# Compressed branch of the attention heads: its bias added by VectorE from the selected branch's table, and each tile of queries takes only the blocks that end within it

## The reference, cut to what matters

```python
end = arange(n_cmp) * CMP_STRIDE + CMP_LEN - 1          # 31 blocks: 31, 47, ..., 511
dist = qpos[:, None] - end[None, :]
vis = dist >= 0
bias = rel_bias[rel_bucket(dist)]
s = einsum('bqgrd,bngd->bgrqn', qg, kc) * SCALE + bias
p = softmax(where(vis, s, NEG_INF)); p = where(any(vis), p, 0)
o = einsum('bgrqn,bngd->bqgrd', p, vc)
```

## Time and profile before

| | us |
|---|---|
| median of three executions | 2705.33 (2705.25 to 2711.46) |
| the profiled execution, whole | 2703.42 |
| its span | 2701.6 |
| PE busy | 2542.1 (94%) |
| DVE busy | 896.3 (33%) |
| ACT busy | 750.1 (28%) |
| POOL busy | 422.2 (16%) |
| stretch of the 8 turns of `heads`, about | 1316 to 2325 |

### The profile page before, as it was taken

How to read it: one execution, slowest core, us unless ns; L and a number is a source line. 1 busy time by engine, 2 the same in 40 slices (tenths; PEclk the granted TensorE clock), 3 DMA queues, 4 the chain that set the end, 5 groups by cost and what they waited for, 6 DMA issues and landing times.

```text
span 2701.6 us, 49851 instructions
## 1 busy us (share of the span) xinstructions
PE 2542.1 (94%) x20936; PEld 2349.6 (87%) x20936; DVE 896.3 (33%) x1560; ACT 750.1 (28%) x1266; POOL 422.2 (16%) x577
## 2 busy tenths in 40 slices
PE   7998999999999999968899999999999999876996
PEld 6987888988999999968899898989899999655996
DVE  1235112221633533322433324242433333332334
ACT  1124111112422411111432324333333333221223
POOL 1002000950000000332311112020202011111000
PEclk9998999999999999989899999999999999987998
DMA  9986776766454365699523232323222232466221
GB/s 322 330 280 220 234 228 197 227 215 216 157 154 140 126 218 180 166 79 113 119 63 89 63 89 66 90 61 92 80 76 82 71 88 64 157 210 247 94 93 64
DMA packets 321990, 395.72 MB, mean 146 GB/s; under 512 B 24846, under 2 KB 283166, under 8 KB 319906
## 3 DMA queue, kind: packets, MB, share of 16 engines
q1 hardware_dynamic: 301650, 327.66, 40.8%
q0 software_dynamic: 20144, 65.12, 8.6%
HBM read 372.03 MB, written 43.72 MB: 154 GB/s over the span
## 4 chain that ended last, share of the span: by engine, by line
PE 85%; DMA 6%; DVE 4%; issue 2%; ACT 2%; SPq 1%; POOL 0%; DVEq 0%; ACTq 0%; POOLq 0%
PE acc L1898 64%; PE work L1819 4%; DMA raw<-in_w_kv 3%; PE out_acc L2073 3%; PE work L1766 2%; PE work L2042 2%; PE work L1807 2%; PE work L2059 1%; PE acc L1766 1%; PE work L2036 1%; PE work L2035 1%; SPq L565 1%; PE out_acc L2070 1%; DMA ada<-in_w_ada 1%; DVE normed L1386 1%
## 5 line engine op out<-in xcount | busy, mean ns | idle before, releaser
L1898 PE MATMUL acc<-h_hi,w_hi 128*128 128x260 f32 x4896 | 1017.1, 289 | 53.8 <-DVE w_lo L1259 42.4
L1898 PE MATMUL acc<-h_hi,w_lo 128*128 128x260 f32 x4896 | 995.5, 285 | 0.0
L1898 PE MATMUL acc<-h_lo,w_hi 128*128 128x260 f32 x4896 | 994.3, 285 | 0.0
L1898 PEld LDWEIGHTS acc<-h_hi,w_hi 128*128 128x128 f32 x4896 | 764.1, 191 | 95.1 <-issue 57.8
L1259 DVE TENSOR_TENSOR w_lo<-raw,w_hi 128x1024 fp32r<-128x1024 f32 (+1 forms) x316 | 403.6, 1278 | 1134.4 <-ACT w_hi L921 1129.6
L1898 PEld LDWEIGHTS acc<-h_hi,w_lo 128*128 128x128 f32 x4896 | 764.8, 191 | 0.0
L1898 PEld LDWEIGHTS acc<-h_lo,w_hi 128*128 128x128 f32 x4896 | 763.7, 191 | 0.0
L921 ACT ACTIVATE w_hi<-raw 128x1024 fp32r<-128x1024 f32 (+1 forms) x316 | 332.5, 1053 | 1209.3 <-PE acc L1898 1147.2
L861 POOL TENSOR_TENSOR probs<-probs,row_stats 128x128 f32<-128x128 f32 (+3 forms) x128 | 111.0, 898 | 475.5 <-DVE row_stats L1612 475.5
L1819 PE MATMUL work<-rows_T_early,w_c_early 128*128 128x124 f32 x960 | 111.9, 275 | 0.7 <-ACT rows_T_early L965 0.7
L1819 PEld LDWEIGHTS work<-rows_T_early,w_c_early 128*128 128x128 f32 x960 | 109.5, 192 | 1.1 <-DVE rows_T_early L1332 1.1
(11 more groups left out here) (319 smaller groups left out, 2010.3 us busy)
## 6 DMA issues: line engine op xcount, KB each, us to landing
ada<-in_w_ada SPq DMA_DIRECT2D x192, 512.0 KB, 4.8
raw<-in_w_in_b SPq DMA_DIRECT2D x128, 512.0 KB, 3.9
raw<-in_w_in_a SPq DMA_DIRECT2D x64, 512.0 KB, 5.0
raw<-in_w_kv SPq DMA_DIRECT2D x48, 512.0 KB, 5.0
raw<-in_w_out_a SPq DMA_DIRECT2D x32, 512.0 KB, 3.6
raw<-in_w_out_b SPq DMA_DIRECT2D x32, 512.0 KB, 3.3
x_scr<-x POOLq DMA_DIRECT2D x2, 4160.0 KB, 14.4
pages_early<-in_cache_k_cmp SPq DMA_DIRECT2D x32, 256.0 KB, 4.1
```

Of the source, the lines that this page charges most:

```text
L1898: last = mm_(out[half][0:n, 0:HT], part[slot][:, kk, cols_], src[:, k, half * HT:(half + 1) * HT], start=(first and part is HI and src is ...
```

## The change

The bias tables of the compressed branch go: the buffer `BC`, its DRAM table `c_scr`, the DMA that writes it and the DMA that loads it in each turn. The loads that a turn waits for are four instead of five. PE's compressed scores are four matmuls a head instead of eight, without the bias, with 7, 15, 23 and 31 columns. DVE fills the probabilities with -1e30, adds the bias to each tile's columns out of `BH` at every 16th column, and takes maximum and difference from SBUF instead of PSUM.

```diff
-        BC = place("bias_cmp", [NCMP, 2, TP])
...
-            pool.dma_start(c_scr, bass.AP(tensor=g_scr.tensor, offset=GLEN + 481, ap=[[2 * GLEN, NH], [-16, NCMP], [1, TP]])).then_inc(s_bscr, 16)
...
-            pool.wait_ge(s_bscr, 16 * (1 + NH // 4))
+            pool.wait_ge(s_bscr, 16 * (NH // 4))
...
-                pool.dma_start(BC[:, :, :], h2(c_scr)).then_inc(hd_in, 16)
...
-                    dve.wait_ge(hd_in, 80 * (i + 1))
+                    dve.wait_ge(hd_in, 64 * (i + 1))
...
                 if u < 2:
-                    sc = S[0][:, 0:NT * NCMP].rearrange("p (t n) -> p t n", n=NCMP)
                     pr = PR[:, 0:NT * NCMP].rearrange("p (t n) -> p t n", n=NCMP)
-                    o(V.tensor_reduce(STAT[:, 0:4], sc, AX.X, ALU.max))
-                    V.tensor_tensor(pr, sc, STAT[:, 0:4].unsqueeze(2).broadcast_to([P, NT, NCMP]), ALU.subtract).then_inc(negm, 1)
+                    o(V.memset(PR[:, 0:NT * NCMP], NEG))
+                    for t in range(NT):
+                        w, at = 8 * t + 7, (3 - t) * P + CL - 1
+                        last = V.tensor_tensor(pr[:, t, 0:w], S[0][:, NCMP * t:NCMP * t + w], BH[:, hh, at:at + CS_ * (w - 1) + 1:CS_], ALU.add)
+                    o(last)
+                    o(V.tensor_reduce(STAT[:, 0:4], pr, AX.X, ALU.max))
+                    V.tensor_tensor(pr, pr, STAT[:, 0:4].unsqueeze(2).broadcast_to([P, NT, NCMP]), ALU.subtract).then_inc(negm, 1)
...
-                    pe.wait_ge(hd_in, 80 * (i + 1))
+                    pe.wait_ge(hd_in, 64 * (i + 1))
...
                     for t in range(NT):
-                        out = S[0][:, NCMP * t:NCMP * t + NCMP]
-                        mm_(out, BC[:, hh, P * t:P * t + P], ident[0:NCMP, 0:NCMP], start=True, stop=False)
-                        last = mm_(out, qs(t), kc, start=False, stop=True)
+                        w = 8 * t + 7
+                        last = mm_(S[0][:, NCMP * t:NCMP * t + w], qs(t), kc[:, 0:w], start=True, stop=True)
```

More of the change, by code:

```diff
@@ L391, in build @@
         b_scr = dram("b_scr", (NH, P, 512))
-        c_scr = dram("c_scr", (NH, NCMP, TP))
         x_scr = dram("x_scr", (P, KT * T))
```

## The result

The changed kernel took 2658.9 us (median of four, 2656.65 to 2664.92) against 2705.29 of the kernel before on the same chip: a ratio of 0.9827, 95% interval 0.9806 to 0.9849, 46.4 us less. The forecast was 2667, range 2661 to 2682. Two later comparisons gave 39.8 us (0.9854, 0.9832 to 0.9877) and 44.9 us (0.983, 0.9813 to 0.9848).

A forecast was written before the change was run, and what follows sets the result against it. PE, with 85% of the chain of waits, was taken as the bound. Scores 28.8 plus clock 9.2 gave 38.0 us off, other terms 0: 2665.4 for the profiled execution, 2667 for the median, range 2661 to 2682.

The forecast's parts named there:

- The scores: PE's compressed scores in `heads`: stretch falls from 2.69 to 0.89 us a head as row alternation goes, saving 28.8 us.
- the bound I gave for the columns: PE's scores: if fewer moving columns pay, 48 columns a head save 0.08 us, 1.3 us in all.
- The clock: PE behind the score stretches: all six falls to half clock go, 6 x 1.53 = 9.2 us; bounds 0 and 9.2.
- DVE: Added fill and adds on DVE: 1.0 us a head, covered with 3.5 us to spare before PE's transposes, cost 0.
- The loads of a turn: Each turn of `heads`: the removed fifth load was needed some 20 us after issue, so dropping it gains nothing.
- Gain 0; nothing of it is left to move: The compressed table's 992 KB DMA, issued at 747.25: PE is busy all 20 us around it, so removal gains 0.
- The windows before 1316 should be as they were: Expected sign in the changed profile: the stages ahead of `heads` keep their times, a change of 0 there.
- The base: Starting level of the kernel before: profiled execution 2703.42 us, with the median 1.9 above it.
- The slower rival: Key/value projection: moved scratch tables lengthen PE's 45.18 us weight wait; decides from 38 us, 84% longer; chance 0.02.

## Why the prediction was right and where it was wrong

**The scores: right.** 28.8 us forecast, 16 x 1.87 = 29.9 measured. The step that carried it, that 0.335 is the price of alternating between 31 and 128 rows, is shown by the run with equal rows. The remaining error of 1.1 us is the pace at few columns, 0.205 a matmul instead of 0.223. With 31 columns throughout it is the same, so the bound I gave for the columns was rightly left out.

**The clock: right.** 9.2 us forecast, all six falls gone, in the eight profiles of kernels with the 0.82 us stretch and no added work on DVE. That it was the long stretch of narrow matmuls is shown, as one without any 31-row matmul brings the falls back: 0 of 16 behind 0.82 us, 2 of 16 behind 2.00, 11 of 16 behind 2.60 at 7 to 31 columns, 6 of 16 behind 2.69 at 31. Length alone does not order these counts, and why 2.60 us had more falls than 2.69 was not tried.

**DVE: right.** 0.69 us a head against my 1.0, and a cover of 3.84 against my 3.5. The run with the long fill confirms the cover to 0.1 us.

**The loads of a turn: right.** Kept alive, they cost nothing.

**"Gain 0; nothing of it is left to move": the step that failed.** I had priced the table's DMA and overlooked what its removal does to addresses, other than as a rival that could only make things slower. The new place makes the first wait for weights shorter, by 5.3 us in the mean of six profiles against six, and the stretch from the pooling output projection to `heads` by about 4. "The windows before 1316 should be as they were" was wrong for the same reason. The mechanism had been named, its sign had not: with no row on it, it belonged in the range on both sides.

**The base was a draw.** I took the median of three, 2705.33, as the level of the kernel before. Over 32 executions it is 2701.5, 3.8 lower. Two profiles of one kernel differ by 6.5 us by the time the pooling output projection begins, so the low end needed this spread as well. Base 3.8, place 4 and scores 1.1 make 8.9 us, where 8.4 lie between 2667.3 and 2658.9. The time missed the range by 2.1 us, so with either the base or the place alone put right it would have lain inside.

**The slower rival's price was not tested.** I let it decide from a wait longer by 84%, so that each us of wait costs one of time. The 45 us on the chain are not all idle time: all of it removed, with the second one, was worth 33 us and not 74. Between the two places of the tables 5.3 us of the first wait went with 4.2 us of the stretch, which is nearer to one for one. No run here made the wait much longer.

## What to carry to other kernels

Group matmuls by their number of contraction rows, and do not use a small matmul against an identity to add a bias between full-height ones. Taken out, each of them gave back 1.87 / 4 = 0.47 us here, about twice the 0.226 that a matmul takes among equals, and the long stretch of narrow matmuls cost the clock as well. Before pricing a wait from the chain, read PE's busy time and its granted clock in the same window. Count a removed or added DRAM table as a move of every table behind it.

## What the runs showed of the hardware that I had not expected

- A 992 KB shift of scratch tables in DRAM, without any traffic of its own, changed a wait for weights under small DMAs from 39 to 41 us to 44 to 47 us (six profiles against six: 39.76, 41.29, 39.33, 40.97, 41.09, 39.06 against 45.18, 44.83, 46.17, 44.11, 47.44, 45.60).
- PE at 100% busy in the records lost its full clock behind 2.6 us of matmuls with 7 to 31 columns, in 11 of 16 cases (0.50 granted in the window shown).
- Eight narrow matmuls took 0.335 us each in turns of 31 and 128 rows and 0.226 each with 31 rows throughout.
- POOL's scaling of 124 columns took 1.33 to 1.45 us behind the start of a two-input instruction of VectorE and 0.39 alone. When it started 0.12 us ahead of that instruction it kept its 0.39.
